# First item's rows gathered ahead of the hand-over between two blocks, and two weight splits instead of five ahead of their transposes

## What is computed

```python
def moe(h, w_router, b_router, w_gu, b_gu, w_down, b_down):
    logits = (hf @ w_router + b_router).astype(jnp.float32)
    top_val, top_idx = lax.top_k(logits, TOP_K)          # 4 of 32
    probs = jax.nn.softmax(top_val, axis=-1)
    ...
    xs = hf[tok_sorted]                                  # rows gathered by expert
    gu = lax.ragged_dot(xs, w_gu, group_sizes) + b_gu[e_sorted]
    gate = jnp.minimum(gu[:, :D_FF], SWIGLU_LIMIT)
    up = jnp.clip(gu[:, D_FF:], -SWIGLU_LIMIT, SWIGLU_LIMIT)
    act = gate * jax.nn.sigmoid(SWIGLU_ALPHA * gate) * (up + 1.0)
    out = lax.ragged_dot(act, w_down, group_sizes) + b_down[e_sorted]
```

## Time and profile before

| | us |
|---|---|
| median of 3 runs | 2127.55 |
| lowest and highest | 2125.33, 2129.04 |
| the profiled execution's own time | 2127.16 |
| its span, first to last instruction | 2125.3 |
| PE busy | 2017.8 (95%) |
| DVE, ACT, POOL busy | 1539.4, 1286.5, 783.6 |

### The profile page before, as it was taken

How to read it: one execution, slowest core, us unless ns; L and a number is a source line. 1 busy time by engine, 2 the same in 40 slices (tenths; PEclk the granted TensorE clock), 3 DMA queues, 4 the chain that set the end, 5 groups by cost and what they waited for, 6 DMA issues and landing times.

```text
span 2125.3 us, 38424 instructions
## 1 busy us (share of the span) xinstructions
PE 2017.8 (95%) x11881; PEld 1508.8 (71%) x11882; DVE 1539.4 (72%) x1997; ACT 1286.5 (61%) x1710; POOL 783.6 (37%) x1016
## 2 busy tenths in 40 slices
PE   5999899999859999999999999999999999999995
PEld 4999776777557676676766678867786676787652
DVE  3633467767867677787776679968797797898557
ACT  2531344454326666686756668768776786878554
POOL 3232466656732232233232223333232232334224
PEclk8999999999969999999999999999999999999997
DMA  8878551224378798897877699999899899999765
GB/s 329 276 286 289 216 164 65 97 96 145 112 264 306 283 338 302 297 342 276 321 282 274 246 325 383 387 351 326 312 379 335 278 366 344 346 380 391 262 213 182
DMA packets 163476, 593.38 MB, mean 279 GB/s; under 512 B 23120, under 2 KB 46621, under 8 KB 127573
## 3 DMA queue, kind: packets, MB, share of 16 engines
q1 hardware_dynamic: 135005, 528.71, 66.0%
q0 software_dynamic: 27440, 62.89, 11.8%
q10 hardware_dynamic: 976, 1.03, 0.2%
HBM read 536.10 MB, written 56.65 MB: 279 GB/s over the span
## 4 chain that ended last, share of the span: by engine, by line
PE 61%; issue 3%; DVE 3%; ACT 2%; DVEq 1%; ACTq 0%; DMA 0%; POOLq 0%
PE pg L2295 10%; PE pg L2296 9%; PE pg L2298 9%; PE py L2254 7%; PE py L2230 6%; PE py L2231 5%; PE py L2234 5%; PE pg L2268 3%; ACT hi L2432 2%; DVE lo L2524 2%; PE pt L2225 1%; PE pt L2219 1%; PE pg L2288 1%; PE pt L2240 0%; PE pg L2402 0%
## 5 line engine op out<-in xcount | busy, mean ns | idle before, releaser
L2295 PE MATMUL pg<-hi,xs 128*128 128x512 f32 x1056 | 432.6, 410 | 0.0
L2296 PE MATMUL pg<-lo,xs 128*128 128x512 f32 x1056 | 412.0, 390 | 0.0
L2524 DVE TENSOR_TENSOR lo<-spare,hi 128x1024 fp32r<-128x1024 f32 x264 | 306.2, 1220 | 82.0 <-ACT hi L2432 79.0
L2524 DVE TENSOR_TENSOR lo<-w_out,hi 128x1024 fp32r<-128x1024 f32 x272 | 313.7, 1218 | 69.4 <-ACT hi L2432 68.1
L2298 PE MATMUL pg<-hi,xs 128*128 128x512 f32 x1056 | 325.7, 390 | 0.0
L2524 DVE TENSOR_TENSOR lo<-raw,hi 128x1024 fp32r<-128x1024 f32 x264 | 314.2, 1220 | 8.4
L2432 ACT ACTIVATE hi<-spare 128x1024 fp32r<-128x1024 f32 x264 | 259.2, 1048 | 43.2 <-PE pg L2298 43.2
L2432 ACT ACTIVATE hi<-w_out 128x1024 fp32r<-128x1024 f32 x272 | 265.4, 1049 | 31.7 <-SPq L2062 25.4
L2432 ACT ACTIVATE hi<-raw 128x1024 fp32r<-128x1024 f32 x264 | 270.5, 1056 | 23.3 <-PE pg L2298 23.3
L2295 PEld LDWEIGHTS pg<-hi,xs 128*128 128x128 f32 x1056 | 198.3, 188 | 71.6 <-issue 14.1
L2298 PEld LDWEIGHTS pg<-hi,xs 128*128 128x128 f32 x1056 | 198.2, 188 | 42.5
(11 more groups left out here) (482 smaller groups left out, 3685.4 us busy)
## 6 DMA issues: line engine op xcount, KB each, us to landing
w_out<-in_w_gu SPq DMA_DIRECT2D x136, 1024.0 KB, 7.0
spare<-in_w_gu SPq DMA_DIRECT2D x132, 1024.0 KB, 10.5
raw<-in_w_down SPq DMA_DIRECT2D x132, 1024.0 KB, 8.9
ada_w<-in_w_ada SPq DMA_DIRECT2D x4, 2048.0 KB
h_tiles<-hTc POOLq DMA_DIRECT2D x8, 1024.0 KB, 8.9
spare<-in_w_ada SPq DMA_DIRECT2D x4, 2048.0 KB
hT<-h_tiles SPq DMA_DIRECT2D x8, 1024.0 KB
w_i<-in_w_in SPq DMA_DIRECT2D x3, 2048.0 KB, 20.2
```

What stands on the lines that cost most here:

```text
L2295: pe.matmul(pg[u][b][:, :], xs[:, kt, 0, :], wh[:, u, :], start=False, stop=False)
L2296: pe.matmul(pg[u][b][:, :], xs[:, kt, 0, :], wl[:, u, :], start=False, stop=False)
L2524: dve.tensor_tensor(lo[q % RING][:, :, :], grain(q % GRAINS), hi[q % RING][:, :, :].bitcast(F32), ALU.subtract).then_inc(s["lo"], 1)
```

## The change

The gather of item 0's rows is taken out of the expert block and issued by POOL as the last instruction of the mixing block, behind waits for the index rows (`vrow_out`), for the stores of the residual rows and of `h2`, and for `h2` itself. Its destination is a new tensor `first_rows` at a fixed place, where the mixing block had the residual rows `xr` and where the expert block has `xg` (64 more columns, `above`, are put in ahead of `xg` for that). Its semaphore lives outside both blocks, so that the clear between them doesn't touch it, and PE's and POOL's waits on `xg` in the expert block wait on it. In the expert block, ACT and DVE split two grains instead of five ahead of the row parts and six instead of three behind them, and PE's second run of identity products is 5 long instead of 10.

```diff
@@ mixing, POOL @@
             list_slots(t, P)
             list_slots(u, T)
             pool.wait_ge(s["listed"], 64 * (TILES + 1))
+            pool.wait_ge(s["vrow_out"], 16 * (1 + P // TAIL))
+            pool.wait_ge(s["x1_out"], 16 * (TILES + 1))
+            pool.wait_ge(s["h2_out"], 16 * (TILES + 2))
+            pool.wait_ge(s["h2"], 2 * TILES + 2)
+            pool.sem_inc(s["met"], 1)
+            pool.indirect_dma_start(keep["first_rows"][:, :], None, scratch["h2"][:, :],
+                                    bass.IndirectOffsetOnAxis(ap=keep["idx"][:, 0:1], axis=0)).then_inc(keep["first_rows_in"], 16)
     s.clear()
@@ experts @@
     s = Signals(nc, "moe")
+    s["xg"] = keep["first_rows_in"]
...
         xs_t = sb("xs_t", [P, KT * TAIL])
+        above = sb("above", [P, 64])
         xg = sb("xg", [P, D])
@@ experts, POOL @@
-            pool.indirect_dma_start(xg[:, :], None, scratch["h2"][:, :],
-                                    bass.IndirectOffsetOnAxis(ap=idx[:, 0:1], axis=0)).then_inc(s["xg"], 16)
             gather_tail()
@@ experts, PE @@
             for half in range(2):
                 transpose_rows(0, half, pt[1 - half])
-            run_in(10)
+            run_in(5)
@@ experts, ACT (DVE the same with split_lo and rows_lo) @@
-            for q in range(5):
+            for q in range(2):
                 split_hi(0, q)
             for half in range(2):
                 rows_hi(0, half, pt[1 - half])
-            for q in range(5, RING):
+            for q in range(2, RING):
                 split_hi(0, q)
@@ build @@
+    FIRST_ROWS = 43968
...
+        with nc.sbuf_tensor("below_rows", [P, FIRST_ROWS], F32), nc.sbuf_tensor("first_rows", [P, D], F32) as first_rows:
+            keep["first_rows"] = first_rows
+        keep["first_rows_in"] = nc.alloc_semaphore("first_rows_in")
```

## The result

The changed kernel takes 2133.35 us (median of 12 runs, 2130.37 to 2136.95), the one before 2127.12 in the same session (12 runs, 2125.33 to 2130.59). The ratio is 1.0026, 95% interval 1.0018 to 1.0033: 4 to 7 us slower. The profiled execution of the changed kernel took 2131.11 us for a span of 2129.2.

The account below looks back on a forecast made before the run. TensorE, busy for 95% of the span, was taken as the bound, with the first bias product as clock. +7.7 us (barrier) − 1.7 (TensorE's way) = +6.0, added to the median 2127.55: 2133.5 us, range 2126.8 to 2136.5.

Parts of the forecast that it names:

- The place: Hand-over from mixing to expert block: whatever moves item 0's first bias product (632.24 us) moves the kernel's end one for one.
- The gather's start: End of mixing block: gather starts 0.86 us behind the index rows' landing (about 618.4), so near 619.3 us.
- The drain: POOL's DRAIN at L107: ends 6.1 to 8.6 us after the engine is free; low end taken, about 626.4 us.
- The first rival: POOL's drain at L107 waits for the gather's landing alone: +3.3 to +4.8 us, 2130.9 to 2132.3; chance 0.25.
- The barrier term: Barrier between the blocks: POOL's drain behind the gather makes TensorE start 7.7 us later.
- TensorE's way: From TensorE's start to the first bias product: 10.0 us in place of 11.74, a gain of 1.7 us.
- the clock's bound: TensorE's first run-in: 5 to 6.5 us depending on when the clock rises, −1 to +0.4 us.
- The rival on the other side: Barrier at L107: drain is free once POOL is, 0 us change (2127.5), or −1.1 with the sequencer further ahead; chance 0.2.
- ACT's later splits: Item 0 of the expert block: rival that late splits reach TensorE, +0.3 to +3.3 us on top; chance 0.05.
- the two readings that I weighed: TensorE's queue before the first bias product: 64 instructions by the skill (gain 2.7 us), or about half (gain 1.7).

Follow-up runs that it names:

- e2: Kernel before with only the splits (five to two) and the run-in products behind the transposes (ten to five) changed, gather in its old place; ratio 0.9993 to before.
- e7: Changed kernel with one more POOL drain ahead of the wait for tile 6's listed slots, where POOL idles; ratio 1.0016 to the kernel before.
- e4: Changed kernel with one more POOL drain right behind the wait for the listed slots, ahead of the gather; ratio 1.0014 to the kernel before.
- e3: Kernel before with one more POOL drain ahead of the block's end, two in a row with no DMA between; ratio 0.9999 to before.
- e11: Kernel before with ACT's and SP's block-end waits moved behind the barrier, 25 run-in products and 5 behind the transposes, no added POOL drain; ratio 1.0002 to before.
- e5: Changed kernel in which POOL waits for the gather's landing before the block ends; ratio 1.0048 to the kernel before.

## Why the prediction was right, and where it was not

- **The place.** Right. The loss arises between the last index load and the first bias product, and neither the moved splits nor the run-in products cost TensorE anything later (e2).
- **The gather's start.** Right: 0.84 us behind the index rows, I had 0.86; the index loads gate it.
- **The drain.** Right in size, wrong in kind. I took the low end of 6.1 to 8.6 us "after the engine is free"; measured are 6.5 us (618.3 to 624.8). But that isn't a fixed time behind POOL's last instruction. It is the landing (621.7) plus half of the work that 112 DMAs leave (3.1 us). That my rule fitted is a matter of this place: with so many DMAs to answer for, all the work counted from POOL's last instruction, 618.3 + 6.2, ends at 624.5, 0.3 us from the measured end. With 9 DMAs since the last drain the rule would have been 2.2 us too high (e7: POOL free at 622.3, end at 626.2), with one 2.7 (e4: 619.1 and 622.5). The first rival, the landing alone, had half of the cause, and my argument against it held: what it leaves out is the 6.1 us at line 107 with everything landed.
- **The barrier term.** I had +7.7 us, it was +8.3 (release 23.5 against 15.2): mis-sized by 0.6, of which 0.4 are the drain (6.5 for 6.1) and 0.2 the gather's later start, since the index rows landed that much later on the clock.
- **TensorE's way.** I had 1.7 us of gain, it was 2.4 (9.4 us in place of 11.7). The run-in took 5.60 us in place of 6.05, inside the clock's bound that I had given; by the spread over the executions above this is chance. And the sequencer passed line 2388 at 632.0, 5.5 us behind the start, not 6.1; from there it was the 3.9 us that I had.
- **The two errors cancel**: 8.3 - 2.4 = 5.9, where I had 7.7 - 1.7 = 6.0. That they do is luck: the sum is better than its terms.
- **The rival on the other side**, a drain that is free once POOL is: its evidence, POOL's 618.7 beside ACT's 618.6, was a coincidence of two waits. e3 shows the drain at its full 6116 ns with nothing to wait for.
- **ACT's later splits**: nothing of it in the changed kernel. ACT's ninth split starts 4.9 us behind the first bias product (I had 5.3), and TensorE's one wait for a split in item 0, ahead of its down products, is 3.9 us, 3.8 before. From the first bias product to the end it took 1493.3 us, 1493.1 before.

On the depth of TensorE's queue the two readings that I weighed can be told apart. The sequencer's record behind the second run-in comes in nearly the same moment as the first transpose, at 632.0 here and at 628.6 with the short first run-in. Between the first run-in and that record the program has 18 passes, 8 transposes and 10 of the second run-in. In all fourteen traces, the kernel before among them (where I had read 17 passes), the weight loads of exactly 16 passes of transposes and run-in begin behind that record. Each is a weight load and a product, so the sequencer gets 16 passes, 32 instructions, ahead of the array. The Trainium skill (TensorE: Matmul & The Clock Gate, section "Architectural detail: the array is 16× 32×32, not 1× 128×128") gives 64 instructions; these traces bear out about half of it.

## What to carry to other kernels

A block's end costs each engine its drain, and POOL's is not free: it waits for its DMAs in flight and does some work for each DMA since its last drain (at this barrier about 0.04 us for a direct and 0.08 for an indirect one; at the kernel's end these prices don't hold, see below). Before a load is moved ahead of a barrier to hide it, ask what the barrier then waits for; a drain where POOL idles takes the work off, but not the flight. Where several waits end within half a microsecond, as ACT's, SP's and POOL's did, removing one shows nothing, and removing all released the barrier 4 us earlier: keep the semaphore past the barrier and wait where the data is used, each use for its own load.

## What was not expected of the hardware

- A POOL drain with all DMAs landed and POOL idle: 0.37 us for 4, 0.69 to 0.71 for 8, 6.116 for 111, 6.197 for 112; the 6.116 is the same to the nanosecond in five kernels. The drains of ACT and SP at the same barrier took 8 and 13 ns, DVE's 0.31 us, and TensorE's 4.07 us, which end with its last product. The Trainium skill (VectorE: DVE Perf Modes, section "The DRAIN you can't avoid") knows drains of about 12 ns on all five engines around a program; here, at a block's end, ACT's and SP's are of that size, the other three are not.
- At the kernel's end POOL's drain stops 8.6 us behind its last product. The expert block has 117 indirect DMAs and 243 direct ones, which at the prices above would be 20 us. This stays open.
- Behind the first bias product, the profiled executions of these kernels differ by several microseconds: 1493.1 to 1496.1 us to the end, and 1499.6 for e11. Only a clock that stops at the first bias product tells changes of 1 to 3 us apart here.
- TensorE's granted clock rose to full no later after 5 run-in products than after 15. With 5 (TensorE's start at 626.3) it was 0.50 from 624 to 628 and 0.85 on average in the next 4 us. With 15 it varied from execution to execution: in e2 (start at 621.2) 0.50 from 620 to 624 and 0.99 in the next 4 us, in e5 (start at 631.0) 0.50 from 632 to 636 and 0.90 in the next 4.
